# The second gating of a group behind the additions of the down product, on VectorE's queue

## The reference, cut to what matters

```python
def conv_ffn(h, buf, w_up, conv_w, conv_b, w_down):
    z = h @ w_up                                   # 1024 -> 2 x 2816
    zc, new_buf = causal_dwconv(z, buf, conv_w)    # 3 taps over the tokens
    gate, up = jnp.split(zc + conv_b, 2, axis=-1)
    return (jax.nn.silu(gate) * up) @ w_down, new_buf

def shortconv_mixer(h, buf, w_in, conv_w, w_out):
    bg, cg, u = jnp.split(h @ w_in, 3, axis=-1)
    y, new_buf = causal_dwconv(cg * u, buf, conv_w)
    return (bg * y) @ w_out, new_buf
```

## Time and profile before

| | |
|---|---|
| median of 3 runs | 1625.99 us |
| lowest, highest | 1624.21, 1626.87 us |
| span of the profiled execution | 1624.3 us |
| TensorE busy | 1547.9 us (95%) |
| VectorE busy | 1058.9 us (65%) |
| GpSimd busy | 512.5 us (32%) |
| ScalarE busy | 458.6 us (28%) |
| mean granted clock of TensorE | 0.984 of full |

### The profile page before, as it was taken

The page is one execution under the profiler, slowest core; times in us unless marked ns, Lnnn a source line. Parts: engine busy times, 40 slices in busy tenths (PEclk is TensorE's granted clock), DMA queues, the critical chain, the costliest instruction groups (busy, mean ns, idle before and its releaser), DMA issues.

```text
span 1624.3 us, 26037 instructions
## 1 busy us (share of the span) xinstructions
PE 1547.9 (95%) x10292; PEld 1522.0 (94%) x10292; DVE 1058.9 (65%) x1313; ACT 458.6 (28%) x717; POOL 512.5 (32%) x221
## 2 busy tenths in 40 slices
PE   6999999999999999999998999998999999999995
PEld 5999998899999999999998999998999999999994
DVE  6556665755956666666767553368966666667667
ACT  4345664443212121212115111115211111121123
POOL 4322220243323333233233333333333323332331
PEclk8999999999999999999999999999999999999997
DMA  5211116222222222221222222212122222222211
GB/s 205 70 61 53 53 53 229 102 66 66 69 70 70 78 65 66 76 76 54 77 78 71 80 68 78 74 59 78 54 77 78 65 77 65 77 64 65 78 37 65
DMA packets 34873, 123.76 MB, mean 76 GB/s; under 512 B 3920, under 2 KB 6864, under 8 KB 33648
## 3 DMA queue, kind: packets, MB, share of 16 engines
q1 hardware_dynamic: 31872, 108.37, 21.2%
q10 hardware_dynamic: 2928, 14.35, 2.3%
HBM read 114.48 MB, written 8.22 MB: 76 GB/s over the span
## 4 chain that ended last, share of the span: by engine, by line
PE 74%; DVE 17%; DVEq 4%; issue 2%; ACT 1%; DMA 0%; POOL 0%; SPq 0%; ACTq 0%
PE ps L401 58%; PE ps L417 8%; DVE hh L972 4%; DVE x L761 3%; DVE y L965 2%; DVE y L961 2%; PE ps L484 2%; PE ps L584 2%; DVEq L1017 1%; DVE sq L728 1%; DVE xl L712 1%; DVEq L1002 1%; PE ps L536 1%; PE ps L691 1%; DVE zp L984 1%
## 5 line engine op out<-in xcount | busy, mean ns | idle before, releaser
L345 POOL TENSOR_TENSOR wl<-raw,wh 128x1024 fp32r<-128x1024 f32 x195 | 485.9, 2498 | 1003.1 <-ACT wh L1173 1003.1
L401 PE MATMUL ps<-xh,wh 128*128 128x328 f32 (+5 forms) x2176 | 506.5, 314 | 15.6 <-DVE xl L712 15.3
L401 PE MATMUL ps<-xl,wh 128*128 128x328 f32 (+5 forms) x2176 | 503.1, 313 | 0.0
L401 PE MATMUL ps<-xh,wl 128*128 128x328 f32 (+5 forms) x2176 | 502.7, 313 | 0.0
L401 PEld LDWEIGHTS ps<-xh,wh 128*128 128x128 f32 x2176 | 389.3, 190 | 18.8 <-issue 9.5
L401 PEld LDWEIGHTS ps<-xl,wh 128*128 128x128 f32 x2176 | 390.2, 190 | 0.0
L401 PEld LDWEIGHTS ps<-xh,wl 128*128 128x128 f32 x2176 | 389.5, 190 | 0.0
L1173 ACT ACTIVATE wh<-raw 128x1024 fp32r<-128x1024 f32 x196 | 204.3, 1055 | 346.6 <-PE ps L401 323.3
L417 PE MATMUL ps<-gh,wh 128*128 128x322 f32 (+1 forms) x800 | 186.3, 314 | 30.3 <-DVE x L761 30.2
L965 DVE SCALAR_TENSOR_TENSOR y<-zp,par,y 128x660 f32<-128x660 f32 (+1 forms) x192 | 185.6, 967 | 26.9 <-issue 22.1
L761 DVE TENSOR_TENSOR x<-ps,x 128x644 f32<-128x644 f32 (+2 forms) x208 | 161.7, 821 | 53.8 <-PE ps L417 28.7
(11 more groups left out here) (154 smaller groups left out, 1153.4 us busy)
## 6 DMA issues: line engine op xcount, KB each, us to landing
raw<-w_units SPq DMA_DIRECT2D x196, 512.0 KB, 3.5
s<-states ACTq DMA_DIRECT2D x4, 1024.0 KB, 5.3
state_sample<-snew ACTq DMA_DIRECT2D x4, 1024.0 KB, 4.1
x<-x_t SPq DMA_DIRECT2D x8, 328.0 KB, 6.5
x<-x_t ACTq DMA_DIRECT2D x1, 2624.0 KB, 11.4
y_t<-x SPq DMA_DIRECT2D x6, 320.0 KB, 2.4
ffn_last<-zl ACTq DMA_DIRECT2D x2, 396.0 KB, 2.4
zc<-ffn_cache ACTq DMA_DIRECT2D x1, 704.0 KB, 4.2
```

What stands on the lines that cost most here:

```text
L345: pool.tensor_tensor(wl[:, j, :, :], raw[:, j, :, :], wh[:, j, :, :].bitcast(F32), ALU.subtract).then_inc(sem["lo_done"], 1)
L401: mm = pe.matmul(ps[:, p, c:c + z - a], w[:, ring, k, :], v[:, k, a:z], start=(k == 0 and w is wh and v is hi), stop=(k == KT - 1 and w is ...
```

## The change

VectorE's queue is reordered; no instruction is added or taken away. In `down` the late gating stands behind the eighth addition instead of between the second and the third; number 9 of each layer keeps the old place (`after=2`). In the mixer the same is done for the products of groups 0 and 1, while the last of the three keeps the old place.

```diff
-        def down(layer, g, i=0, late=None):
+        def down(layer, g, i=0, late=None, after=KT):
 
             for m in range(KT):
-                if m == 2 and late:
+                if m == after:
                     late()
                 add_to_x(take(("down", layer, g, m), i), m, FIRST_Z[layer] + STEP)
+            if after == KT:
+                late()
             dve.drain()
...
                     for m in range(KT):
-                        if m == 2:
+                        if m == 2 and g == MIX_G - 1:
                             gate_mix(2 * g + 1)
                         add_to_x(take(("mix_out", g - 1, m)), m, FIRST_MIX)
+                    if g < MIX_G - 1:
+                        gate_mix(2 * g + 1)
                     dve.drain()
...
-            down(layer, 9, late=lambda: gate_z(layer, 10, 3, f0 + 20))
+            down(layer, 9, late=lambda: gate_z(layer, 10, 3, f0 + 20), after=2)
```

## The result

The changed kernel takes 1589.2 us (median of 4 runs, 1584.3 to 1590.6), the kernel before 1626.4 beside it: a ratio of 0.9752, 95% interval 0.9729 to 0.9775. That is 37 us less by the medians and 37 to 44 by the interval. The medians and intervals of this document leave out two runs that were slow throughout, at a lower granted clock: one of e10's four (1904.0 us) and one of the kernel before beside e5 to e8 (1709.9 us).

The account below looks back on a forecast made before the run. TensorE was taken as the bound, busy 95% of the span, with 18 waits for VectorE's additions; 30.2 + 18 x 0.16 = 33.1 us removed, other terms zero, so 1626.0 - 33.1 = 1592.9 us, range 1590 to 1602.

Parts of the forecast that it names:

- What goes: Down products: with the gating behind, addition 2 ends near 579.0, before its buffer is wanted at 581.8; the wait goes.
- What one wait costs: 18 down products: each wait costs its idle time plus 0.16 us of lost matmul overlap, 33.1 us in all.
- upper bound: Gain from the 18 waits: not above 35.8 us, the weight loads' idle time for the same line.
- The low end of the range: Whole kernel: lower end of the likeliest case's own range, 1590.2 us, with 35.8 us less.
- What is late next: Down products: addition 0 ends at 577.4, its buffer is wanted at 578.2; 0.8 us in hand, no new wait.
- rival A: Lag carried through GpSimd's subtractions to later VectorE instructions returns 0.3 to 1 us per product: 1598 to 1611, chance 0.12.
- Where the gating goes: Behind addition 7: the gating meets two GpSimd subtractions, VectorE's 6.41 us of idle time covers it; costed at nothing.
- T + 5 to T + 7.7: When the moved gating ends, T being the next unit's first matmul; that unit is late by at most 0.3 us.
- the unknown: Cast L976 in the gating: either slips through (end near T + 5) or takes turns with GpSimd (near T + 7.7).
- The mixer: Mixer's two edited products: weight loads show 0.31 us of waiting, worth 0.2 at most, taken as 0.
- The three products left alone: Number 9 of each layer and number 2 of the mixer: no TensorE wait, nothing to gain or lose.
- Rivals B and C: B: addition 0 over 2.6 us later, 1644, chance 0.02; C: an equal wait for weights replaces the removed one, 1626, 0.04.

Follow-up runs that it names:

- e10: Changed kernel plus four memsets between additions 1 and 2 of the 18 FFN products: 1611.3 us, ratio 0.9889 to the kernel before.
- e5: Changed kernel plus six memsets between additions 1 and 2 of the 18 FFN products: 1656.7 us, ratio 1.0181 to the kernel before.
- e8: The kernel before, run again with no edit: 1631.7 us.
- e9: Changed kernel plus five memsets between additions 1 and 2 of the 18 FFN products: 1631.2 us, ratio 1.0018 to the kernel before.
- e1: The changed kernel, run again with no edit: 1589.9 us, ratio 0.9771 to the kernel before.
- e11: The change in the 18 FFN products alone, the mixer as in the kernel before: 1590.6 us, ratio 0.9783 to the kernel before.
- e2: Against the kernel before, the gating two places later, between additions 3 and 4, in the 20 places: 1592.1 us, ratio 0.9783.
- e7: The change in layer 0's nine products alone, layer 1 and the mixer as in the kernel before: 1609.7 us, ratio 0.9885 to the kernel before.
- e4: Against the kernel before, the gating one place earlier, between additions 0 and 1: 1673.5 us, ratio 1.0278.
- e6: Changed kernel plus ten memsets between additions 1 and 2 of the 18 FFN products: 1739.9 us, ratio 1.0695 to the kernel before.

## Why the prediction was wrong

**What goes: right.** Addition 2 freed its buffer in time, the waits of L417 went from 30.2 us to none, a product from 16.20 to 14.35 us and a group from 44.75 to 42.9. e9 shows that the wait is the cause: as long a wait made of memsets gives the whole time back.

**What one wait costs: the step that failed,** by its size. "The last pair before it starts at 581.45 and the next at 583.57 ... 1.82 us lost for 1.66 of idle time, 0.16 more. Over 18: 30.2 + 18 x 0.16 = 33.1 us." The 18 products' times fell by 294.0 - 256.4 = 37.6 us in the two traces; the medians differ by 37.3. Two things are missing in the 33.1.

First, the half-clock stretches behind the waits: 2 of the 18 products had one in the trace that the prediction was made from, 3.1 us by e8's 1.55 each. They can be seen without the clock, too: behind 447.80 the last 24 matmuls of the product took 5.2 us where others take 3.7.

Second, a wait costs more than the spacing in front of it shows: 37.6 less 3.1 is 34.5, or 0.24 us more than the idle time for each wait instead of 0.16. TensorE's timeline and its weight loads' (PEld) in the chosen product, kernel before, show where the rest is:

```profile
583.57 0.56 PE L417 MATMUL ps<-gh,wh 128*128 128x322 f32 x2 [1.66 <-DVE x L761]
583.97 0.46 PE L417 MATMUL ps<-gl,wh 128*128 128x322 f32 x2
...
583.57 0.30 PEld L417 LDWEIGHTS ps<-gh,wh 128*128 128x128 f32 x2 [1.92 <-DVE x L761]
```

The pair behind the wait is followed after 0.40 us, not 0.30: 0.1 us more, 1.92 in all. That is the idle time of the weight loads, and from weight load to weight load this product takes 16.27 us against 14.34, 1.93 more (the window of 16.20 in the earlier trace rows starts 0.2 us into the product). In the 18 products the weight loads' idle time is 34.9 us, which is 35.8 less three short ones elsewhere. So the number that the prediction took for an upper bound was the price of the waits, and as a bound of the gain it failed too, since it knew nothing of the clock. The low end of the range, 1590.2, was worked out from it and came out too high. That the median lies just outside the range rather than just inside is partly chance: the changed kernel measured 1589.9 in e1, and 1590.6 without the mixer's edits in e11.

The Trainium skill (TensorE: Matmul & The Clock Gate, Part 1) says that TensorE's clock passes either every pulse or half of them, and depends on how busy the engine has been. The traces agree that there are two levels in these products, 1.00 and 0.50, and that in these products the lower one comes only with waits, late in them or behind them.

**What is late next: right.** Addition 0, with time in hand: in the product shown it came 0.5 us later than before and nothing waited for it. So rival A's mechanism did occur, a lag that is carried to GpSimd's subtractions and back to L961, but it used up 0.5 of the 0.8 us in hand. In one product, the second of layer 1, 0.3 us of the weight loads' idle time appears, and e2, where the gating doesn't collide, is 0.5 us shorter in its products. That is all that rival A was worth.

**Where the gating goes: right.** Two instructions waited for one subtraction each, at the upper of the two values (T + 5 to T + 7.7; 583.1 is 7.7 us behind the unit's first matmul), and VectorE's idle time took it up. The first to wait was L973, which the prediction didn't name; L978, which it named beside the cast, took its 0.83 us. The cast was the unknown, and it does take part in the turns, as the Trainium skill has it (SBUF — State Buffer, Who interferes with whom): 2.54 us against 0.50.

**The mixer:** 0.3 us in e11's comparison, where the prediction had 0.2 at most and took 0; the weight loads' 0.31 was again the price. **The three products left alone** have no wait of TensorE's matmuls as forecast; the weight loads' idle time in number 9 of layer 0 went from 0.2 to 0.4 us. **Rivals B and C** didn't occur.

**Open:** the two traces differ by 41.8 us of span, 4.2 more than the products account for. Half-clock stretches lie there too (two in the attention stage in the trace of before, none in that of the changed kernel; at the end of layer 0 one twice as long as in the changed kernel), and other runs have them at other places in either kernel. Outside the 18 products the changed kernel takes 1326.0 us in its first trace and 1332.9 in e1, the kernel before 1330.3 and 1335.8 in e8. So this part varies as much between traces of one kernel as between the two; I take it to be chance, but no experiment here was aimed at it. What decides, behind waits of one length, which products get a stretch is open as well.

## What to carry to other kernels

When one engine adds up results for another, put any other work of its queue where no buffer is waiting to be freed: behind the last of the results costs nothing if the engine is idle there, and here two places later than the old one would have done as well. A wait of TensorE costs more than its matmuls' idle time: price it by the idle time of the weight loads, or by the time of a whole stage with and without it, in two windows that start and end on the same instruction, and read the granted clock behind every wait, not in one chosen place. A time that depends on such stretches also needs a range that holds the spread of the runs, 10 us here, not only that of the sum.

## What the runs showed of the hardware

- The clock of TensorE was halved, for some 3.5 us, at 2 of 18 waits of 1.7 us on average (two traces), 2 of 9 of 1.7 us (e7), 4 of 18 of 1.7 us (e9), 11 of 18 of 2.6 us (e5), 15 of 18 of mostly 2.7 to 3.3 us (e4), and all 18 of 5.9 us (e6, in 17 for twice as long, from some 2 us before the wait's end); at none of 17 waits of 0.9 us (e10). One stretch of the usual length costs about 1.5 us.
- A wait in the down products cost what the weight loads sat idle, 0.26 us more for each wait than the matmuls did (34.9 us against 30.2 in 18): 21.0 us of product time against 21.1 in e10, where no stretch adds to it.
- In the changed kernel a VectorE instruction of 0.28 us (L973) and a cast of 0.50 us (L976), both on SBUF alone, took 2.49 and 2.54 us when a subtraction of GpSimd ran; memsets into SBUF didn't: 0.60 us each in e5 from 586.53 on, while a subtraction ran from 586.27 for 2.40.
- Additions that read PSUM, L761, were never stretched: 0.81 to 0.83 us in all of 208 in either kernel, also beside GpSimd's subtraction at 568.63 in the changed kernel.
